# The residual stream goes to the output ahead of the merging stage, and GpSimd adds the last product's pieces by accumulating transfers

## The reference, cut to what matters

```python
y_a = (mixed * pool_scale.astype(jnp.float32)).astype(x.dtype) * jax.nn.silu(z_a)
p_a = jnp.einsum('bsc,cd->bsd', y_a, w_proj_pool.astype(y_a.dtype))
p_b = jnp.einsum('bsc,cd->bsd', y_b, w_proj_mlstm.astype(y_b.dtype))
merged = jax.nn.sigmoid(g_a + b_merge[0]) * p_a + jax.nn.sigmoid(g_b + b_merge[1]) * p_b
out = jnp.einsum('bsd,de->bse', merged, w_out.astype(merged.dtype))
return x + rms_norm(out, norm_post_g)
```

## Time and profile before

| | us |
|---|---|
| median of 3 runs | 1658.86 (1657.21 to 1660.49) |
| profiled execution, its own time | 1662.71 |
| its span in the profile | 1660.9 |
| PE busy | 1638.0 (99%) |
| DVE / ACT / POOL busy | 719.4 / 645.8 / 650.7 |
| HBM read / written | 145.41 MB / 2.10 MB |

### The profile page before, as it was taken

How to read it: one execution, slowest core, us unless ns; L and a number is a source line. 1 busy time by engine, 2 the same in 40 slices (tenths; PEclk the granted TensorE clock), 3 DMA queues, 4 the chain that set the end, 5 groups by cost and what they waited for, 6 DMA issues and landing times.

```text
span 1660.9 us, 22225 instructions
## 1 busy us (share of the span) xinstructions
PE 1638.0 (99%) x7820; PEld 1342.0 (81%) x7820; DVE 719.4 (43%) x1149; ACT 645.8 (39%) x1001; POOL 650.7 (39%) x278
## 2 busy tenths in 40 slices
PE   7999999999999999999999999999999999999997
PEld 6888888887887668888888888878888888888886
DVE  4333330205534775433333033576688741563222
ACT  5323322323424773332233133464444532444433
POOL 3444444444332024444444444443233324444444
PEclk9999999999999999999999999999999999999999
DMA  4322322325222002223223223222112112332322
GB/s 169 101 96 94 101 90 100 101 88 178 77 76 77 2 2 78 93 96 101 90 99 101 88 101 109 93 78 90 64 63 76 63 64 89 115 106 96 101 90 100
DMA packets 41955, 149.28 MB, mean 90 GB/s; under 512 B 4784, under 2 KB 4912, under 8 KB 41648
## 3 DMA queue, kind: packets, MB, share of 16 engines
q1 hardware_dynamic: 40112, 142.37, 25.8%
q10 hardware_dynamic: 1792, 6.21, 1.1%
HBM read 145.41 MB, written 2.10 MB: 89 GB/s over the span
## 4 chain that ended last, share of the span: by engine, by line
PE 51%; issue 37%; POOL 10%; DVE 1%; ACT 1%; POOLq 0%; DVEq 0%; ACTq 0%
PE ps L517 12%; PE ps L519 12%; PE ps L518 12%; POOL w_lo L472 10%; PE ps L625 2%; PE ps L623 2%; PE ps L624 2%; PE ps L773 1%; PE ps L787 1%; PE ps L797 1%; PE ps L1130 1%; PE ps L1128 1%; PE ps L1129 1%; PE ps L704 0%; DVE scr L2264 0%
## 5 line engine op out<-in xcount | busy, mean ns | idle before, releaser
L472 POOL TENSOR_TENSOR w_lo<-w_raw,w_hi 128x1024 fp32r<-128x1024 f32 x262 | 635.9, 2427 | 914.9 <-ACT w_hi L1164 907.9
L1164 ACT ACTIVATE w_hi<-w_raw 128x1024 fp32r<-128x1024 f32 x260 | 275.6, 1060 | 876.4 <-PE ps L519 643.0
L517 PE MATMUL ps<-h_hi,w_hi 128*128 128x512 f32 x1040 | 408.8, 393 | 2.4 <-POOL w_lo L472 1.8
L519 PE MATMUL ps<-h_hi,w_lo 128*128 128x512 f32 x1040 | 406.2, 391 | 0.0
L518 PE MATMUL ps<-h_lo,w_hi 128*128 128x512 f32 x1040 | 406.0, 390 | 0.0
L517 PEld LDWEIGHTS ps<-h_hi,w_hi 128*128 128x128 f32 x1040 | 196.2, 189 | 46.2 <-issue 2.8
L519 PEld LDWEIGHTS ps<-h_hi,w_lo 128*128 128x128 f32 x1040 | 196.0, 188 | 41.5
L518 PEld LDWEIGHTS ps<-h_lo,w_hi 128*128 128x128 f32 x1040 | 196.3, 189 | 39.8
L517 PE MATMUL ps<-n_hi,w_hi 128*128 128x512 f32 x512 | 204.6, 400 | 1.0 <-ACT qk_pad L1476 1.0
L519 PE MATMUL ps<-n_hi,w_lo 128*128 128x512 f32 x512 | 200.4, 391 | 0.0
L518 PE MATMUL ps<-n_lo,w_hi 128*128 128x512 f32 x512 | 199.9, 390 | 0.0
(11 more groups left out here) (327 smaller groups left out, 1850.9 us busy)
## 6 DMA issues: line engine op xcount, KB each, us to landing
w_raw<-in_units SPq DMA_DIRECT2D x262, 512.0 KB, 3.3
x<-in_x SPq DMA_DIRECT2D x4, 512.0 KB, 7.1
w<-in_w ACTq DMA_DIRECT2D x1, 2048.0 KB, 7.7
out<-scr SPq DMA_DIRECT2D x8, 256.0 KB, 2.0
scr<-proj ACTq DMA_DIRECT2D x8, 128.0 KB, 3.7
inv_count<-in_inv_count ACTq DMA_DIRECT2D x1, 1024.0 KB, 4.8
const<-in_const SPq DMA_DIRECT2D x1, 772.0 KB, 9.8
cbias<-in_cbias ACTq DMA_DIRECT2D x1, 512.0 KB, 9.5
```

The lines of the kernel that those rows point to most:

```text
L472: nc.gpsimd.tensor_tensor(w_lo[:, slot, :], w_raw[:, slot, :], w_hi[:, slot, :].bitcast(F32), ALU.subtract).then_inc(w_lo_done, 1)
L517: nc.tensor.matmul(ps[:, bank, :], whi, hi[:, k, :], start=(n == 0), stop=False)
L519: mm = nc.tensor.matmul(ps[:, bank, :], wlo, hi[:, k, :], start=False, stop=(n == DC - 1))
L1164: nc.scalar.activation(w_hi[:, slot, :], w_raw[:, slot, :], ACT.Copy).then_inc(w_hi_done, 1)
```

## The change

In words:

- A new function `stream_out` on ACT, called between `pooled` and `merge_a`, waits for `xt_done` and issues four DMAs, one per token group, that write the stream `x` to the output tensor. One DMA writes 128 rows of 4096 bytes. Its source in a partition is eight stretches of 512 bytes, one for each feature group.
- POOL's four additions (L501) and VectorE's four additions (L2269) are gone, and so are SP's eight output DMAs (L462).
- POOL instead waits until the four stream DMAs have landed, and then for each piece n in order waits for its product (`sum_done`) and issues a DMA that adds `scr[:, n, :]` to the output tensor in place (`accum_op=ALU.add`). SP still waits for all eight.
- VectorE no longer waits for `xt_done` in `output`.

```diff
-POOL_ADDS = 4
-        x_out, x_out_pool = sem("x_out"), sem("x_out_pool")
+        x_out = sem("x_out")
-        def x_piece(n):
+        def out_piece(n):
             tt, half = PIECES[n]
-            return x[:, 4 * half:4 * half + 4, tt * P:(tt + 1) * P]
-
-        def sum_piece(n):
-            return scr[:, n, :].rearrange("p (c t) -> p c t", c=4)
+            return out[tt * P:(tt + 1) * P, half * T:(half + 1) * T]
@@ SP, after the loop over the weights
-            for n, (tt, half) in enumerate(PIECES):
-                if n < POOL_ADDS:
-                    sp.wait_ge(x_out_pool, n + 1)
-                else:
-                    sp.wait_ge(x_out, n - POOL_ADDS + 1)
-                sp.dma_start(out[tt * P:(tt + 1) * P, half * T:(half + 1) * T], scr[:, n, :]).then_inc(out_sem, 16)
             sp.wait_ge(out_sem, 16 * len(PIECES))
@@ POOL, after the last tails
-            for n in range(POOL_ADDS):
+            pool.wait_ge(x_out, 16 * TT)
+            for n in range(len(PIECES)):
                 pool.wait_ge(sum_done, n + 1)
-                nc.gpsimd.tensor_tensor(sum_piece(n), sum_piece(n), x_piece(n), ALU.add).then_inc(x_out_pool, 1)
+                pool.dma_start(out_piece(n), scr[:, n, :], accum_op=ALU.add).then_inc(out_sem, 16)
@@ ACT
+            def stream_out():
+                act.wait_ge(xt_done, DC)
+                for tt in range(TT):
+                    act.dma_start(out[tt * P:(tt + 1) * P, :].rearrange("p (c t) -> p c t", c=DC),
+                                  x[:, :, tt * P:(tt + 1) * P]).then_inc(x_out, 16)
+
             pooled()
+            stream_out()
             merge_a()
@@ VectorE, output()
-                dve.wait_ge(xt_done, DC)
-                    if half == 1 and n >= POOL_ADDS:
-                        for done in (n - 1, n):
-                            dve.wait_ge(sum_done, done + 1)
-                            nc.vector.tensor_tensor(sum_piece(done), sum_piece(done), x_piece(done), ALU.add
-                                                    ).then_inc(x_out, 1)
```

## The result

The changed kernel takes 1670.15 us (median of 6 runs, 1667.32 to 1674.61) against 1658.93 (1657.21 to 1660.99): a ratio of 1.0066, 95% interval 1.0051 to 1.0081. It is slower by 11.2 us, outside the range that was predicted.

What follows compares the result with a forecast made beforehand. PE, busy 1638.0 of 1660.9 us, was taken to bound the kernel up to the last product, then the end's chain of waits. Tail +2.2 and stall +0.5 made +2.7 on 1658.86: 1661.5 us, range 1657.3 to 1667.2.

Steps and rivals of the forecast that it cites:

- VectorE without its additions: End stage: without additions queued ahead of group 3, VectorE's last product ends 1.93 us earlier, at 1655.25.
- The issue on POOL (c): End stage: POOL's issue of one adding DMA, taken as 1.0 us between bounds of 0.33 and 1.66.
- The transfer of an adding piece (d = 1.4): End stage: DMA time per adding piece, 1.4 us if reading limits, between bounds of 0.70 and 2.1.
- the tail's +2.2: End stage: eight adding transfers in a row from 1651.05 end the span at 1663.1, 2.2 us later than before.
- The four stream issues on ScalarE: Between pooled and merge_a: four DMA issues on ACT's queue delay the next weights' head, stalling PE 0.5 us.
- I take 0.5: Stream's place: PE stall chosen in us, from 0.77 per issue; bounds were no stall and 4.1.
- the price that the text gave for this case: Stream's place, issues at 1.66 us each: PE stall of 4.1 us, plus about 1.6 for a dropped PE clock.
- The slack of 1.70: Stream's place: us between POOL's tail done at 1530.93 and PE wanting that unit at 1532.63.
- this rival: Stream's place: the stream's issues hold ACT, stall 4.1 us, with the tail +6.3, 1665.2, or 1666.8 with clock; chance 0.27.
- The rivals: Stream issues hold ACT, chance 0.27; adding queue slower than two reads, 0.19; adding costs nothing in the transfer, 0.13.
- the issue-bound case: End stage: adding free in the transfer, d = 0.70 and c = 1.0, POOL's issues set the end; -1.3 us, 1657.5.
- The stream beside the weights: Stream's place: 2 MB sharing DMA engines with weight loads, taken as no cost, within a slack of 3.8 us.

Runs made afterwards that it cites:

- run 7: Changed kernel with the stream DMAs spread, its eight adding transfers made into SBUF tensor x instead of the output; 1663.46 against 1660.65 us, ratio 1.0015.
- run 6: Changed kernel with the stream DMAs spread, four adding transfers of 512 KB in place of eight of 256 KB; 1664.53 against 1660.65 us, ratio 1.0026.
- Run 2: Changed kernel without the stream DMAs and POOL's wait for them, the eight adding transfers kept; 1664.01 against 1660.42 us, ratio 1.0022.
- run 3: Changed kernel with plain transfers from GpSimd in place of the adding ones; 1662.71 against 1660.42 us, ratio 1.0020.
- run 5: Changed kernel with each of the four early stream DMAs in 128 long stretches instead of 1024, same bytes; 1664.75 against 1660.65 us, ratio 1.0026.
- run 4: Changed kernel with the four stream DMAs spread, one behind every second z unit of the pooled stage; 1663.14 against 1660.42 us, ratio 1.0015.
- run 10: Against the kernel before: transfers add pieces 0 to 3, VectorE adds 4 to 7 behind all its products, GpSimd none; 1662.21 against 1660.73 us, ratio 1.0008.
- runs 1 to 4: The first of these: kernel before plus the four early stream DMAs, its additions and output DMAs kept; 1666.43 against 1660.42 us, ratio 1.0034.

## Why the prediction was wrong, point by point

- **VectorE without its additions: right.** 1.93 us were foretold for the last product; in the trace it comes 1.99 earlier, counted from the first.
- **The issue on POOL (c): not what binds.** 1.0 was taken. The first adding issue takes 1.02, the later ones up to 2.10, but they overlap and start 0.55 to 0.71 after each other where a product is ready. A plain issue there takes 0.54 to 0.71.
- **The transfer of an adding piece (d = 1.4): the term mis-sized.** Half rate is right in size: with SBUF on both sides 1.48 (run 7), with 4096-byte rows 1.43 (run 6). That the second read is the reason no run shows; run 7 shows only that reading HBM isn't. As the change has it, a piece takes 1.64, and the first packet moved 2.2 us after the first product's end and not 1.5: 0.6 pass before POOL's first issue starts, a term that the sum doesn't have. Eight times 0.24 and 0.7 make 2.6 of the 2.7 us by which the tail's +2.2 fell short of +4.9. Run 2 shows this loss alone, run 3 shows it gone with the adding. By the sentence of the Trainium skill ("Collectives: The Full Stack", section "The bandwidth ceiling: the fold count and why AG ≠ RS ≠ AR") that an adding transfer runs at half rate for its second read, said there of rings between cores, the piece would be 1.4; the traces have 2.0 to 2.4 times the plain 0.70, so the rule holds as a lower bound here.
- **The four stream issues on ScalarE: the step that failed.** The prediction put four issues at 0.5 us of stall in all and no loss of clock. This "I take 0.5" rested on a mean of 0.77 per issue from eight DMAs of 64 rows, and on loads whose issue did not wait for their packets. The issues took 6.12 us together, and the price that the text gave for this case (4.1 for the stall, 1.6 for the clock) was met: 3.7 and 1.7. The slack of 1.70 was nearly right too: by it run 5's 2.89 us of issues give 0.3 of stall, and 0.5 was measured. What was wrong was the price taken for an issue, at most 0.77 where it was 1.53 on the mean, and with it a chance of only 0.27 for this rival. The argument from the first loads of the earlier trace rows compared DMAs of at most 256 stretches with four of 1024; run 5 shows that the count matters.
- **The rivals were treated as exclusive.** Each had its own chance, with the other's term left at the forecast. Both costs came: 5.4 + 4.9 = 10.3, against 11.2 timed (8.5 to 13.4). Nothing joined them, and nothing kept them apart, and a range to 1667.2 left no room for both. Its ends don't quite follow from the text either: the issue-bound case was 1657.5 there, not 1657.3, and 1667.0 lies in the middle of 1666.8 and 1667.2.
- **The stream beside the weights: right.** The loads landed within their slack, at most 4.9 us after their issue; the stream at other places shows no cost in the trace (run 4). The text's price of 0.1 us per packet, 25.6 us in all, was far too high: 4160 packets took 60.2% of 12 us, 7.2.

Open: why the adding transfers run at 150 GB/s at first and at 200 later. In the changed kernel the rise comes after GpSimd's issues, but in run 10 the last of four issues ends at 1652.24 and the rate stays at 92 to 143 GB/s until 1654.8, so the issuing alone isn't the reason. In SBUF (run 7) the rate is nearly even.

## What to carry to other kernels

A DMA's issue isn't always cheap: here four DMAs of a thousand short stretches back to back held the issuing engine until nearly half of their packets were under way, and singly they didn't. So count stretches, and spread such DMAs (or give them to an engine on whose queue nothing waits, which no run tried). An adding transfer cost the DMA engines twice a plain one or more, so it saves nothing where the last transfers decide the end. And where two costs of a change are unknown and independent, add their upper cases before closing the range.

## What the runs showed of the hardware that was not expected

- Four DMAs of 512 KB with 1024 stretches each, issued back to back on ScalarE's queue: 0.65, 0.7 to 0.9, and 3.79 us for the fourth. One at a time: 0.55. With 128 stretches each: 0.36 to 1.19. The fourth of the first kind ended when 1921 to 1983 of 4160 packets had started, in three traces.
- Adding transfers of 256 KB: 1.53 to 1.65 us of all DMA engines a piece in HBM (four traces), 1.48 in SBUF (one); plain 0.70.
- Plain and adding transfers together (run 10): the plain ones' landing doubles from 2.0 to 4.1 us, and they end 2.6 us after the adding ones.
- The issue of a DMA on GpSimd: 1.02 to 2.10 us with adding, 0.54 to 0.71 without; start to start 0.55 to 0.71 with both where a product is ready.
- VectorE's addition of two SBUF operands took 1.35 us beside GpSimd's and 0.68 alone.
- The end stages of traces that share them agree within 0.2 us (12.06 and 12.05; 16.95, 16.82 and 16.87), but run 5, on another chip than runs 1 to 4, has 16.15. Spans differ by several us: the granted clock fell to its half level for 3.4 us (once 6.8) at one to four of the same four places, near 25, 462, 600 and 1105 us, a different choice in each execution. A difference of a few us has to be read within a stage.
